# Two-layer hybrid decoder step: matmuls that walk their moving operand backwards, weight rows of 136 columns, tiles at a fixed offset from the weights modulo 256, and the second norm's sum one step later

## The reference

```
def trunk_layer(x, ...):
    h = rmsnorm(x, norm1)
    qa, ka, va, hb, gate_b, gate_c, qc, fc, ic, og, zg = split_in(h @ w_in)   # 1024 -> 6400 columns
    ya = dilated window attention of 6 heads over 3 windows    # small products, softmax
    yb = gate_b * conv3(gate_c * hb)
    yc = gated linear recurrence (HGRN2) of 4 heads, normed, * silu(og)
    g = sigmoid(zg + b_gate)
    mix = g[0] * (ya @ w_pa) + g[1] * (yb @ w_pb) + g[2] * (yc @ w_pc)
    x = x + mix @ w_o
    h2 = rmsnorm(x, norm2)
    x = x + square(relu(h2 @ w_up)) @ w_down                  # 1024 -> 4096 -> 1024
    return x, new caches and states
```

## Time and profile before

| | |
|---|---|
| median of 3 runs | 808.7 us |
| the profiled execution | 808.39 us |
| its span, first to last instruction | 806.6 us |
| granted TensorE clock, mean share of full speed | 0.998 |
| TensorE busy | 798.4 us (99%) |
| VectorE, ScalarE, GpSimd busy | 572.8, 435.1, 277.6 us |
| moved by DMA | 199.88 MB, mean 248 GB/s |

### The profile page before, as it was taken

How to read it: one execution, slowest core, us unless ns; L and a number is a source line. 1 busy time by engine, 2 the same in 40 slices (tenths; PEclk the granted TensorE clock), 3 DMA queues, 4 the chain that set the end, 5 groups by cost and what they waited for, 6 DMA issues and landing times.

```text
span 806.6 us, 17621 instructions
## 1 busy us (share of the span) xinstructions
PE 798.4 (99%) x6756; PEld 787.5 (98%) x6756; DVE 572.8 (71%) x776; ACT 435.1 (54%) x625; POOL 277.6 (34%) x246
## 2 busy tenths in 40 slices
PE   9999999999999999999999999999999999999996
PEld 8999999999999999999999999999999999999996
DVE  7978898577877666554587788966797766645552
ACT  6664567544566665344354637664455666644442
POOL 3599393055700000122149927702663000001220
PEclk9999999999999999999999999999999999999999
DMA  8797879968567588767557968997765857687751
GB/s 326 221 339 286 298 242 292 264 228 303 183 209 251 197 290 289 248 239 248 193 174 200 389 241 291 273 261 247 268 230 198 270 188 253 241 282 247 249 208 54
DMA packets 126035, 199.88 MB, mean 248 GB/s; under 512 B 19642, under 2 KB 115690, under 8 KB 118506
## 3 DMA queue, kind: packets, MB, share of 16 engines
q1 hardware_dynamic: 124682, 196.48, 73.7%
q10 hardware_dynamic: 1296, 2.61, 0.8%
HBM read 191.17 MB, written 51.90 MB: 301 GB/s over the span
## 4 chain that ended last, share of the span: by engine, by line
PE 98%; DVE 1%; ACT 0%; ACTq 0%; issue 0%; DVEq 0%
PE main L689 29%; PE main L690 28%; PE main L691 28%; PE small L691 1%; PE small L689 1%; PE small L690 1%; PE small L705 1%; PE small L734 1%; PE small L748 1%; PE main L674 1%; PE main L675 0%; PE main L678 0%; PE small L781 0%; PE main L665 0%; PE small L916 0%; DVE h_lo L1295 0%
## 5 line engine op out<-in xcount | busy, mean ns | idle before, releaser
L1031 ACT ACTIVATE w_hi<-raw 128x1024 fp32r<-128x1024 f32 (+1 forms) x256 | 266.4, 1042 | 230.1 <-PE main L691 137.1
L1279 DVE TENSOR_TENSOR w_lo<-raw,w_hi 128x1024 fp32r<-128x1024 f32 (+1 forms) x256 | 342.1, 1337 | 61.2 <-ACT w_hi L1031 59.7
L689 PE MATMUL main<-h_hi,w_hi 128*128 128x264 f32 x1248 | 357.4, 286 | 0.0
L690 PE MATMUL main<-h_lo,w_hi 128*128 128x264 f32 x1248 | 353.6, 283 | 0.0
L691 PE MATMUL main<-h_hi,w_lo 128*128 128x264 f32 x1248 | 353.4, 283 | 0.0
L689 PEld LDWEIGHTS main<-h_hi,w_hi 128*128 128x128 f32 x1248 | 235.1, 188 | 3.0 <-DVE w_lo L1279 1.3
L690 PEld LDWEIGHTS main<-h_lo,w_hi 128*128 128x128 f32 x1248 | 235.2, 188 | 0.1
L691 PEld LDWEIGHTS main<-h_hi,w_lo 128*128 128x128 f32 x1248 | 234.0, 188 | 0.0
L689 PE MATMUL main<-a_hi,w_hi 128*128 128x264 f32 x512 | 145.3, 284 | 0.0
L690 PE MATMUL main<-a_lo,w_hi 128*128 128x264 f32 x512 | 145.0, 283 | 0.0
L691 PE MATMUL main<-a_hi,w_lo 128*128 128x264 f32 x512 | 145.0, 283 | 0.0
(11 more groups left out here) (245 smaller groups left out, 1038.4 us busy)
## 6 DMA issues: line engine op xcount, KB each, us to landing
raw<-in_w_in SPq DMA_DIRECT2D x48, 1024.0 KB, 5.8
raw<-in_w_up SPq DMA_DIRECT2D x32, 1024.0 KB, 5.3
raw<-in_w_down SPq DMA_DIRECT2D x32, 1024.0 KB, 5.3
out_kvs<-in_cache SPq DMA_DIRECT2D x48, 512.0 KB
out_kvs<-in_cache SPq DMA_DIRECT2D x32, 496.0 KB
raw<-in_w_o SPq DMA_DIRECT2D x8, 1024.0 KB, 6.1
raw<-in_w_br SPq DMA_DIRECT2D x8, 768.0 KB, 6.7
gates<-q_scratch SPq DMA_DIRECT2D x4, 768.0 KB, 7.6
```

What stands on the lines that cost most here:

```text
L689: pe.matmul(out[:, 0:TOK], wh, rh, start=start and k == 0, stop=False)
L690: pe.matmul(out[:, 0:TOK], wh, rl, start=False, stop=False)
L1031: act.activation(w_hi[:, slot(l, u), 0:k, :], raw_of(u, k), ACT.Copy).then_inc(w_hi_ready, 1)
L1279: dve.tensor_tensor(w_lo[:, slot(l, u), 0:k, :], raw_of(u, k), w_hi[:, slot(l, u), 0:k, :].bitcast(F32), ALU.subtract).then_inc(w_lo_ready, 1)
```

## The change

Four things. The tiles of the weights get rows of 136 columns, of which 128 are used. Unused filler tiles (`before_h` and others) move h, gates, y_hi and y_lo so that, with the longer rows, h, a, mix and y all start 192 bytes past the weights modulo 256. Every split product reads its moving operand, and writes its output, from column 263 down to column 0. The sum of squares for the second norm is issued after unit 1 of up instead of inside it. The same elements are multiplied and summed.

```
+LINE = 8
...
-        w_hi = sb("w_hi", [P, RING, KT, P], F32R)
-        w_lo = sb("w_lo", [P, RING, KT, P], F32R)
+        w_hi_rows = sb("w_hi_rows", [P, RING, KT, P + LINE], F32R)
+        w_lo_rows = sb("w_lo_rows", [P, RING, KT, P + LINE], F32R)
         x = sb("x", [P, KT, TOK])
+        sb("before_h", [P, 6 * LINE])
         h_hi = sb("h_hi", [P, KT, TOK], F32R)
...
+        sb("before_gates", [P, 7 * LINE])
         with ExitStack() as early:
             gates = sb("gates", [P, N_GATE, TOK], stack=early)
...
+            sb("before_y_hi", [P, 4 * LINE], stack=early)
             y_hi = sb("y_hi", [P, BT, TOK], F32R, stack=early)
+            sb("before_y_lo", [P, 2 * LINE], stack=early)
             y_lo = sb("y_lo", [P, BT, TOK], F32R, stack=early)
...
+        w_hi, w_lo = (t[:, :, :, 0:P] for t in (w_hi_rows, w_lo_rows))
...
+            def product(out, w, rhs, start, stop):
+
+                return pe.matmul(out[:, TOK - 1::-1], w, rhs[:, ::-1], start=start, stop=stop)
...
-                    pe.matmul(out[:, 0:TOK], wh, rh, start=start and k == 0, stop=False)
-                    pe.matmul(out[:, 0:TOK], wh, rl, start=False, stop=False)
-                    last = pe.matmul(out[:, 0:TOK], wl, rh, start=False, stop=stop and k == nk - 1)
+                    product(out, wh, rh, start and k == 0, False)
+                    product(out, wh, rl, False, False)
+                    last = product(out, wl, rh, False, stop and k == nk - 1)
...
+                    unit(slot(l, u), main[bank_of(l, O_UP + j)], h_hi, h_lo, 0, KT, per_k=per_k).then_inc(w_used, 1)
                     if j == 1:
-                        per_k = lambda k: sum_squares(l, "norm2", 1) if k == 2 else None
-                    unit(slot(l, u), main[bank_of(l, O_UP + j)], h_hi, h_lo, 0, KT, per_k=per_k).then_inc(w_used, 1)
+                        sum_squares(l, "norm2", 1)
```

More of the change, by code:

```diff
@@ L659, in first_units @@
                         for u in us:
-                            pe.matmul(main[u][:, 0:TOK], w_hi[:, u, k, :], h_hi[:, k, :], start=k == 0, stop=False)
-                            pe.matmul(main[u][:, 0:TOK], w_hi[:, u, k, :], h_lo[:, k, :], start=False, stop=False)
+                            product(main[u], w_hi[:, u, k, :], h_hi[:, k, :], k == 0, False)
+                            product(main[u], w_hi[:, u, k, :], h_lo[:, k, :], False, False)
                     pe.wait_ge(piece_lo, i + 1)
@@ L664, in first_units @@
                         for k in ks:
-                            mm = pe.matmul(main[u][:, 0:TOK], w_lo[:, u, k, :], h_hi[:, k, :], start=False,
-                                           stop=k == KT - 1)
+                            mm = product(main[u], w_lo[:, u, k, :], h_hi[:, k, :], False, k == KT - 1)
                         if k == KT - 1:
@@ L673, in unit_lo_last @@
                 for k in range(KT):
-                    pe.matmul(out[:, 0:TOK], w_hi[:, u % RING, k, :], h_hi[:, k, :], start=k == 0, stop=False)
-                    pe.matmul(out[:, 0:TOK], w_hi[:, u % RING, k, :], h_lo[:, k, :], start=False, stop=False)
+                    product(out, w_hi[:, u % RING, k, :], h_hi[:, k, :], k == 0, False)
+                    product(out, w_hi[:, u % RING, k, :], h_lo[:, k, :], False, False)
                 pe.wait_ge(w_lo_ready, u + 5)
                 for k in range(KT):
-                    last = pe.matmul(out[:, 0:TOK], w_lo[:, u % RING, k, :], h_hi[:, k, :], start=False,
-                                     stop=k == KT - 1)
+                    last = product(out, w_lo[:, u % RING, k, :], h_hi[:, k, :], False, k == KT - 1)
                 return last
```

## The result

Before 808.56 us (median of 13 runs), after 809.88 (13 runs): a ratio of 1.0029, 95% interval 1.0019 to 1.0039. The change costs 1.3 us; the forecast was 40 us faster. The rival "no effect on the pitch" had given 812, and for its sake the range, 752 to 813, holds the result.

A forecast was written before the change was run, and what follows sets the result against it. TensorE, busy 99% of the span, was taken as the bound, at 0.1208 us a product. 808.4 - 46.4 (new pitch) + 3.6 (wait) + 2.4 (lost cover) = 768.0, or 768.3 for the median; range 752 to 813.

The forecast's parts named there:

- no effect on the pitch: Rival: the loss belongs to the product, addresses only redistribute it; only the moved sum costs, 812 us; chance 0.11.
- (a): Longer weight rows and fillers: a constant 192-byte offset for every k; with the reversed walk, 0.113 us a product, 46.4 us saved.
- (b): Operand and output walked backwards: streams meet less often; with the constant offset, 0.113 us a product, 46.4 us saved.
- the milder rival: Only the offset counts, reversing gives nothing: pitch between 0.116 and 0.1208, say 0.1185 us, time 799 us; chance 0.13.
- the third rival: Moving operand catches up with the load and follows its pace: 0.135 us a product, 896 us; chance 0.14.
- Step (c): Second norm's sum moved in up: TensorE waits before unit 3, 3.6 us lost in two layers, 3.2 at the old pitch.
- Step (d): VectorE, full from 100 to 130 us, can't make low halves faster: 2.4 us lost, bounds 0 and 4.2.
- Step (e): ScalarE and VectorE writing weight rows with gaps, and DMAs coming 5% closer together, were counted at nothing.
- Caught behind the loads: Rival: running the same way, the moving operand follows the load's pace, 0.135 us a product, 896 us; chance 0.14.

The follow-up runs named there:

- e14: The kernel before with 252 instead of 264 columns in the three products of a unit; 785.29 us, one execution.
- e8: The kernel before with 240 instead of 264 columns in the three products of a unit; 768.55 us, one execution.
- e4: The kernel before with only the walk of operand and output reversed, old rows and tiles, sum in its old place; 808.48 us, ratio 1.0000.
- e9: The kernel before with each load taking 64 of the 128 weight columns, products still of 264 columns; 806.69 us, one execution.
- e5: The changed kernel with the sum back inside unit 1 of up and a float32 product of 64 columns behind it; 806.1 us, ratio 0.9965.
- e12: e5 with other fillers: h at 0, a and mix at 128 past the weights, y still at 192; 810.62 us, ratio 1.0025 against before.
- e1: The kernel before with only the second norm's sum moved behind unit 1 of up; 812.1 us, ratio 1.0055.
- e6: The changed kernel with the sum back inside unit 1 of up and a float32 product of 8 columns behind it; 806.12 us, ratio 0.9965.
- e2: The changed kernel with the sum back inside unit 1 of up, layout and reversed walk kept; 812.6 us, ratio 1.0049 against before.

## Why the prediction was wrong

**What bounds the kernel** was right: TensorE's pitch, and each nanosecond of it weighs 6 us, less what cover is lost: e14 and e8 bear it out (23 us for 5.0 ns, 40 for 8.7).

**Steps (a) and (b), the new pitch, failed.** 0.113 was forecast, 0.1203 or 0.1225 measured. The premise was that the 11 ns above one column a pulse come from the load meeting the moving operand in SBUF, so that a better meeting would give them back. The steps do depend on the address, as was seen: with a constant offset they repeat after one k or two instead of eight. But the short and the long steps before make up a mean that gives nothing back for a better meeting. e4 turned the direction around, e9 took half the load away, and the mean stayed at 0.1208 and 0.1205 to 0.1208; e14 shows the same 10.8 ns at 252 columns. The 0.11 of the earlier trace rows was taken as what a clean product costs; it was the short half of a pair. The argument held against the rival in the text, "the 0.13, repeated in two tiles", proves an effect of the address on single steps, not on their mean. The six products of the earlier trace rows, which I held against the milder rival, were the better witness (0.120 by rows of two decimals, 0.119 by the starts to the nanosecond): no stretch of 48 products of 264 columns was below 0.120 in any run. In which direction a load walks, which I had assumed, is still unknown. Nor did a run leave the load out altogether, so a fixed cost of changing the weights isn't excluded as the source of the 10.8 ns.

Of the saving, 46.4 us, the quick pattern gives 5,952 x 0.00055 = 3.3 us where it holds; the slow one takes 0.0017 a product.

From the rule quoted with the rival "no effect on the pitch" (the Trainium skill, SBUF — State Buffer, section "SBUF: two separate sides": TensorE waits on no other engine there) I drew that layout can't matter. For the mean that is nearly right, and gave the right forecast. It is not exact: single steps before differ by 14 ns with the address (0.116 to 0.130), and means by 2 ns (e5's down at 192 past the weights, 0.1203; e12's at 128, 0.1225). Whether that is a wait at SBUF no run shows. The gap of 2.5 ns a product (the Trainium skill, TensorE: Matmul & The Clock Gate, section "Back-to-back issue gap") isn't reached in this kernel: it is 10.8. And walking PSUM backwards, feared under the third rival on the ground of a rule on non-contiguous patterns (the Trainium skill, PSUM — Partial Sum Buffer, Specifications (TRN2)), costs nothing here: e4, 1.0000.

**Step (c), the wait, was right.** 1.62 us a layer at the old pitch forecast; measured 1.63 from the last product before to the first after it, beyond a normal step. Not foreseen: the first step of a restarted stream is 0.1 longer. In all 3.4 for the two layers against 3.2, and 3.6 by time in e1.

**Step (d), cover that runs out,** didn't come up, since the pitch hardly fell. e14 and e8 show that it was undersized: 6.7 us lost at 5.0 ns less and 11.5 at 8.7, where I had 2.4 at 7.8. It named the low halves of the weights; most of the loss lies in other work of VectorE that TensorE comes to need: the small products of w_in first, then `mix_lo`. Even with the pitch forecast, the time would have been about 808.7 - 46.4 + 3.6 + 10 = 776 (an estimate between these two runs).

**Step (e)** held: no wait on ACT or DMA that reaches TensorE appeared in after, and its DMA share in the two windows of 150 us is 0.75 and 0.73 against 0.74 and 0.71.

**The rival that came** is "no effect on the pitch", 812 at 0.11. Its size was good to 2 us; what it lacks are the two patterns. That the range holds the result is owed to this rival, not to the forecast's sum. "Caught behind the loads" didn't occur.

## What to carry to other kernels

Where a repeated step varies with the address, take the mean over the whole period before pricing its removal: a short step beside a long one is no proof that all can be short. What a stream costs above one column a pulse is cheap to test first: cut the columns and the load by themselves and see which of the two moves it; here it is 10.8 ns of the product at 252 and 264 columns, and the load of 128 columns at 192 and 240. And when a sum or another small product is moved, look at the pitch of the hundreds of products behind it, not at the gap alone.

## What the runs showed that was not expected

- With a constant offset a product stream has several steady paces, and keeps the one with which it starts as long as the distance from the weights stays (e12 changed pace where the tile changed). With the same instructions and addresses, up and down ran at 0.1203 or 0.1225 us a product from the restart to the end of the layer; with a product of 8 columns behind the sum it was the quick one, by their times in all six runs of e6 (805.87 to 806.95); without it the slow one, in all five of e2 (812.09 to 812.90). What in the start picks the pace is open.
- While the offset goes through all eight multiples of 32, the mean is 0.12083, forwards and backwards, whatever the start (the branch units, with six of the eight, have 0.1214 in both); with constant offsets means of 0.1203, 0.1214, 0.1225 and 0.1247 were seen.
- Beside a load of 128 weight columns a product takes 112.1 ns at 240 columns and still 111.7 at 192; with a load of 64, 192 columns took 88.6, 8.6 ns above one column a pulse. Why less than 10.8 is open.
- Taking half of the load away left the steps varying with k (0.115 to 0.127 in e9), so the variation isn't the length of the load. What makes it wasn't found.
